# A feed-forward stage by seven half products for each pair of weight blocks, and an output projection in three token parts

## The chip, the core and the metric

The kernel runs on one core of a Trainium2 chip. The metric is device time in microseconds (us) of one execution; the kernel before took 2178.95 us (median of 3 runs, 2177.84 to 2180.29). TensorE (PE in the rows) multiplies, VectorE (DVE), ScalarE (ACT) and GpSimd (POOL) do elementwise work, and the queue of SyncE (SP) issues most transfers.

## The reference

One decoder layer in float32 for 1024 tokens of width 1024: token mixing (stick-breaking attention and retention, gated), a norm, attention into a memory of 256 rows, a norm, and this stage, the only one that the change rewrites:

```python
f = x @ w_ffn_in[l]                                   # 1024 -> 2 x 2816
ff = (jax.nn.silu(f[..., :FFN_HIDDEN]) * f[..., FFN_HIDDEN:]) @ w_ffn_out[l]
x = layer_norm(DN_ALPHA * x + ff, ln3_g[l], ln3_b[l])
```

## The kernel before

Everything is kept transposed: 128 channels on the partitions, tokens along the free dimension. `x_hi` and `x_lo` hold the 1024 channels as 8 tiles of [128, 1024]. Precision comes from splitting: a float32 value is a rounded part (hi, type fp32r) and the rest (lo), and each product is three matmuls, hi by lo, hi by hi and lo by hi, summed in PSUM. So each weight block of [128, 1024] (512 KB, 8 contraction tiles of 128x128) must be split before use. Before, POOL does this alone: `w_hi` by a multiplication with one (L280), `w_lo` by a subtraction (L283). Blocks arrive in a list in the order of use; SP loads them into two halves of `w_raw` (`stream`, L247 to L251), the next as soon as POOL has split the last of that slot.

The feed-forward stage has 22 hidden tiles of 128 channels, in three parts of 8, 7 and 7 (`FFN_PARTS`). For each hidden tile PE makes the gate half and the other half (2 blocks, each 8 contraction tiles by 2 token halves by 3 matmuls of 512 columns: 48), then ACT takes the silu from PSUM (L1176), DVE multiplies (L1607), ACT rounds to `a_hi` (L1178) and DVE subtracts to `a_lo` (L1609). After each part, 8 output blocks are multiplied with the part's hidden tiles in `a_hi` and `a_lo` and added to `acc`. That is 22 x 96 = 2112 matmuls inwards and 22 x 48 = 1056 outwards, all of 512 columns.

The norm before the stage (`n2`) has its totals summed by POOL and DVE, and its first half of tokens normalised, then the second: per 512 columns DVE centres (L1483) and scales (L1513), ACT applies gain and bias (L1076) and rounds (L1079), POOL subtracts (L301). PE starts the stage's first two blocks on parts as they come (`as_normed`, L722 to L726). The last norm (`n3`) does all 1024 tokens after the last matmul and stores 16 parts.

Of the kernel before, what the change touches and what calls it, by code (L numbers as in the profile page):

```python
# [26 lines left out]
ALU = mybir.AluOpType  # L27
# [5 lines left out]
P = 128  # L33
# [13 lines left out]
FFN_PARTS = (8, 7, 7)  # L47
# [13 lines left out]
RU, XU = 10, 6  # L61
STEPS = SB_PAIRS * QT
# [11 lines left out]
def layer_program(nc, xT, memT, stream8, stream7, params, rope, consts, ret_branch, outT):  # L74
    ctx = ExitStack()
    with ctx:
# [6 lines left out]

        x_hi = sb(ctx, "x_hi", [P, KT, SEQ], F32R)
# [10 lines left out]
        with ExitStack() as st:  # L95
            stick_set(st, 1)
        acc = sb(ctx, "acc", [P, KT, SEQ])
# [9 lines left out]
        ln_ones = sb(ctx, "ln_ones", [P, P], F32R)  # L107

# [36 lines left out]
        with ExitStack() as st:  # L145
# [7 lines left out]
            with ExitStack() as s2:  # L153
                silu_h = sb(s2, "silu_h", [P, SEQ])
                hidden = sb(s2, "hidden", [P, SEQ])

        with ExitStack() as st:
            y_out = sb(st, "y_out", [P, KT, SEQ])
        with ExitStack() as st:
# [5 lines left out]
            with ExitStack() as s2:  # L165
                ln_mean2, ln_rstd = sb(s2, "ln_mean2", [P, SEQ]), sb(s2, "ln_rstd", [P, SEQ])
                ln_t = sb(s2, "ln_t", [P, 4, HALF])
                ln_x = sb(s2, "ln_x", [P, 4, HALF])
                inv_col = sb(s2, "inv_col", [P, 2, 4])
# [48 lines left out]
        silu_read, hid_hi, hid_lo = sem("silu_read"), sem("hid_hi"), sem("hid_lo")  # L218
        scaled_odd, y_ready, out_stored = sem("scaled_odd"), sem("y_ready"), sem("out_stored")

        class Norm:

            def __init__(self, tag, residual):
# [3 lines left out]
                 self.centered, self.scaled) = (  # L227
# [3 lines left out]
                        "std", "turned", "inverted", "rstd", "centered", "scaled"))  # L231
                if residual:
                    self.a_hi, self.a_split, self.added, self.affine, self.hi, self.done = (
                        sem(f"{tag}_{n}") for n in ("a_hi", "a_split", "added", "affine", "hi", "done"))
                else:
                    self.rstd_copied = sem(f"{tag}_rstd_copied")

        n1, n2, n3 = Norm("n1", True), Norm("n2", True), Norm("n3", False)
# [5 lines left out]
        def _(sp):  # L244
# [20 lines left out]
            for q in range(2 * KT):  # L265
                hf, k = divmod(q, KT)
                sp.wait_ge(y_ready, q + 1)
                sp.dma_start(outT[k * P:(k + 1) * P, half(hf)], y_out[:, k, half(hf)]).then_inc(out_stored, 16)
            sp.wait_ge(out_stored, 16 * 2 * KT)
# [3 lines left out]
        def _(pool):  # L273
# [22 lines left out]
            def normed_lo(m, qs):  # L296

                for q in qs:
# [3 lines left out]
                                       ).then_inc(m.done, 1)  # L302

# [92 lines left out]
            residual(n2, U_MO, CH_MO, False, D, True)  # L396
            single(CH_FFN + 1)
            normed_lo(n2, range(2 * KT))
            split(CH_FFN + 2, 142 - CH_FFN - 2, 8 * P)
            split(142, 8, 7 * P)  # L400
            split(150, 14, 8 * P)
            split(164, 2, 7 * P)
            residual(n3, U_FFN + 60, 164, True, 7 * P, False)
            for q in range(1, 2 * KT, 2):
                hf = q // KT
                pool.wait_ge(n3.centered, q + 1)
                pool.wait_ge(n3.rstd_copied, hf + 1)
                pool.tensor_tensor(ln_t[:, q % 4, :], ln_t[:, q % 4, :], ln_rstd[:, half(hf)], ALU.mult
# [1320 lines left out]
```

## Time and profile before

| what | value |
|---|---|
| median of 3 runs | 2178.95 us |
| the profiled execution | 2180.05 us |
| its span (first to last instruction) | 2178.1 us |
| PE busy | 2059.9 us, 95% |
| POOL busy | 991.1 us, 46% |
| DVE busy | 825.3 us, 38% |
| ACT busy | 521.3 us, 24% |
| mean granted TensorE clock | 0.979 of full |
| transfers | 116.34 MB, mean 53 GB/s |

Busy time is a union over an engine's instructions. Successive matmuls overlap in the records: a matmul's own duration holds its way through the array, so the cost of one among many is the distance between two starts, not its duration. PEclk is the granted clock as a share of 2.4 GHz.

### The profile page before, as it was taken

How to read it: one execution, taken by the hardware profiler on the slowest of the kernel's cores; microseconds unless marked ns; L12 is line 12 of the kernel's file. 1: busy time of each engine (PE TensorE's matmuls, PEld its weight loads, DVE VectorE, ACT ScalarE, POOL GpSimd, SP SyncE). 2: the span in 40 equal slices, each digit the busy share in tenths (PEclk: the TensorE clock that was granted, in tenths of full speed). 3: DMA queues.
4: the chain of work that ended last, by engine and by line, in shares of the span. 5: the costliest groups of instructions: out<-in, count | busy, mean ns of one | idle time of the engine just before them, and what ended most of it. 6: DMA issues, size and time to landing. Idle time of an engine off the chain costs nothing.

```text
span 2178.1 us, 25755 instructions
## 1 busy us (share of the span) xinstructions
PE 2059.9 (95%) x10216; PEld 1702.2 (78%) x10216; DVE 825.3 (38%) x839; ACT 521.3 (24%) x732; POOL 991.1 (46%) x497
## 2 busy tenths in 40 slices
PE   7999999999999999999889989899999999999995
PEld 6888888788777777877678877678888888888884
DVE  5647466300166656144553324542122212112115
ACT  2413224210154555110252221151100000000013
POOL 4232242333354445346775426763344433433375
PEclk9999999999999999999999999899999999999997
DMA  4021020112100000311211111101111111111112
GB/s 187 24 84 65 32 86 20 68 67 77 48 22 28 20 20 30 116 49 39 68 59 58 67 39 39 49 29 48 48 48 48 48 48 44 53 48 48 45 42 77
DMA packets 33349, 116.34 MB, mean 53 GB/s; under 512 B 3728, under 2 KB 5136, under 8 KB 32272
## 3 DMA queue, kind: packets, MB, share of 16 engines
q1 hardware_dynamic: 27648, 93.56, 12.8%
q10 hardware_dynamic: 5648, 22.02, 2.7%
q8 instruction: 39, 0.64, 0.1%
q14 instruction: 14, 0.11, 0.0%
HBM read 107.18 MB, written 8.39 MB: 53 GB/s over the span
## 4 chain that ended last, share of the span: by engine, by line
PE 86%; DVE 8%; issue 2%; ACT 2%; POOL 1%; DMA 0%; POOLq 0%; DVEq 0%; ACTq 0%; SPq 0%
PE unit L437 23%; PE unit L443 23%; PE unit L441 23%; PE aux L602 2%; PE aux L608 2%; PE aux L606 2%; PE aux L415 2%; PE aux L417 1%; PE aux L416 1%; PE aux L562 1%; PE unit L551 1%; PE unit L415 1%; PE unit L417 1%; PE unit L416 1%; DVE ln_t L1483 1%
## 5 line engine op out<-in xcount | busy, mean ns | idle before, releaser
L280 POOL TENSOR_TENSOR w_hi<-w_raw,one 128x1024 fp32r<-128x1024 f32 (+1 forms) x130 | 245.1, 1885 | 888.7 <-PE unit L437 888.7
L437 PE MATMUL unit<-x_lo,w_hi 128*128 128x512 f32 x1440 | 563.3, 391 | 13.3 <-POOL w_lo L294 11.0
L443 PE MATMUL unit<-x_hi,w_lo 128*128 128x512 f32 x1440 | 561.3, 390 | 0.0
L441 PE MATMUL unit<-x_hi,w_hi 128*128 128x512 f32 x1440 | 561.1, 390 | 0.0
L437 PEld LDWEIGHTS unit<-x_lo,w_hi 128*128 128x128 f32 x1440 | 270.8, 188 | 72.5 <-POOL w_lo L294 11.0
L283 POOL TENSOR_TENSOR w_lo<-w_raw,w_hi 128x1024 fp32r<-128x1024 f32 (+1 forms) x130 | 322.1, 2478 | 10.2
L443 PEld LDWEIGHTS unit<-x_hi,w_lo 128*128 128x128 f32 x1440 | 270.7, 188 | 57.0
L441 PEld LDWEIGHTS unit<-x_hi,w_hi 128*128 128x128 f32 x1440 | 270.9, 188 | 55.5
L437 PE MATMUL unit<-a_lo,w_hi 128*128 128x512 f32 x608 | 240.2, 395 | 9.7 <-DVE a_lo L1395 9.7
L443 PE MATMUL unit<-a_hi,w_lo 128*128 128x512 f32 x608 | 239.2, 393 | 0.0
L441 PE MATMUL unit<-a_hi,w_hi 128*128 128x512 f32 x608 | 237.2, 390 | 0.0
L1607 DVE TENSOR_TENSOR hidden<-unit,silu_h 128x1024 f32<-128x1024 f32 x22 | 26.9, 1225 | 355.2 <-PE unit L443 355.2
L387 POOL TENSOR_TENSOR beta<-beta,stick 128x128 f32<-128x128 f32 (+7 forms) x64 | 77.1, 1205 | 151.6 <-DVE stick L1332 151.6
L437 PEld LDWEIGHTS unit<-a_lo,w_hi 128*128 128x128 f32 x608 | 114.6, 188 | 35.9 <-DVE a_lo L1395 9.1
L443 PEld LDWEIGHTS unit<-a_hi,w_lo 128*128 128x128 f32 x608 | 114.6, 188 | 26.1
L441 PEld LDWEIGHTS unit<-a_hi,w_hi 128*128 128x128 f32 x608 | 114.5, 188 | 25.6
L1332 DVE TENSOR_TENSOR_SCAN stick<-stick 128x128 f32<-128x128 f32 (+7 forms) x64 | 106.2, 1661 | 49.8 <-ACT stick L934 49.8
L1176 ACT ACTIVATE silu_h<-unit 128x1024 f32<-128x1024 f32 x22 | 22.6, 1027 | 331.2 <-PE unit L443 331.2
L1430 DVE SCALAR_TENSOR_TENSOR acc<-x_hi,unit 128x1024 f32 (+1 forms) x22 | 26.9, 1221 | 160.8 <-PE unit L443 160.8
L1178 ACT ACTIVATE a_hi<-hidden 128x1024 f32 x22 | 23.4, 1062 | 244.8 <-DVE hidden L1607 244.8
L602 PE MATMUL aux<-x_lo,w_hi 128*128 128x512 f32 x192 | 81.4, 424 | 0.3 <-DVE sk_lo L1347 0.3
L1609 DVE TENSOR_TENSOR a_lo<-hidden,a_hi 128x1024 f32 x22 | 66.6, 3028 | 29.4 <-ACT a_hi L1178 29.4
(258 smaller groups left out, 3252.2 us busy)
## 6 DMA issues: line engine op xcount, KB each, us to landing
w_raw<-stream SPq DMA_DIRECT2D x156, 512.0 KB, 3.3
rope_sb<-rope ACTq DMA_DIRECT2D x8, 1024.0 KB, 6.8
w_raw<-stream SPq DMA_DIRECT2D x16, 448.0 KB, 3.2
acc<-xT ACTq DMA_DIRECT2D x8, 512.0 KB, 9.5
ret_branch<-acc ACTq DMA_DIRECT2D x8, 512.0 KB, 2.6
acc<-ret_branch ACTq DMA_DIRECT2D x8, 512.0 KB, 7.9
outT<-y_out SPq DMA_DIRECT2D x16, 256.0 KB, 2.0
mem_raw<-memT ACTq DMA_DIRECT2D x1, 1024.0 KB, 5.4
```

The source lines that it names most:

```text
L280: pool.tensor_tensor(w_hi[s][:, 0:width], w_raw[:, s, 0:width], one[:].to_broadcast([P, width]), ALU.mult).then_inc(w_hi_done, 1)
L283: pool.tensor_tensor(w_lo[s][:, 0:width], w_raw[:, s, 0:width], f32(w_hi[s][:, 0:width]), ALU.subtract).then_inc(w_split, 1)
L387: pool.tensor_tensor(beta[g % 2][:, hd, 0:n], beta[g % 2][:, hd, 0:n], stick[:, hd, SEQ - n + 1:SEQ + 1], ALU.mult).then_inc(w_ready, 1)
L415: pe.matmul(out, l_hi, r_lo, start=start, stop=False, skip_group_check=True)
L416: pe.matmul(out, l_hi, r_hi, start=False, stop=False, skip_group_check=True)
L417: return pe.matmul(out, l_lo, r_hi, start=False, stop=stop, skip_group_check=True)
L437: x = pe.matmul(out, w_hi[s][:, wk], lo[:, k, cols], start=first, stop=False, skip_group_check=True)
L441: pe.matmul(out, w_hi[s][:, wk], hi[:, k, cols], start=False, stop=False, skip_group_check=True)
L443: last = pe.matmul(out, w_lo[s][:, wk], hi[:, k, cols], start=False, stop=(k == kts - 1), skip_group_check=True)
L602: x = pe.matmul(aux[:, 3, :], w_hi[s][:, wk], x_lo[:, k, half(hf)], start=(k == 0), stop=False, skip_group_check=True)
L1332: dve.tensor_tensor_scan(left[:, ::-1], left[:, ::-1], left[:, ::-1], 1.0, ALU.mult, ALU.bypass).then_inc(stick_scanned, 1)
L1609: dve.tensor_tensor(a_lo[:, bass.ds(j, 1), :].rearrange("p a t -> p (a t)"), hidden[:], f32(a_hi[:, bass.ds(j, 1), :].rearrange("p a t -> ...
```

## The change

The two weight blocks of hidden tile p (rows: gate, other) are cut into two contraction halves, and x into contraction halves and token halves. The 2 x 2 block product is made by Winograd's form of Strassen's method: seven products of [128 x 512] by [512 x 512] in place of eight, each 4 contraction tiles by 3 matmuls of 512 columns. Four of the seven weight forms are sums of quarters (`weight_sum`, DVE); four of the x forms are sums too and are made once, during the second norm (`turn`, `turn_hi_parts`, `turn_lo`): 16 sums on DVE, 16 roundings on ACT, 8 subtractions on POOL and 8 on DVE. The sum of two halves replaces one quarter of `x_hi`. Results are put together from PSUM: ACT copies four products to `held`, DVE makes four sums, ACT the silu, DVE the product, and each finished hidden tile is stored to a DRAM tensor `hidden_store`. The normed x is stored to `mid_x`.

The output projection is turned round: for token parts of 384, 384 and 256 columns, it goes over all 22 hidden tiles, with all eight output tiles open in the eight PSUM banks, 24 matmuls of the part's width for each hidden tile. `KEPT` is empty, so each part loads and splits each of the 22 output blocks anew: 66 loads of 512 KB, 66 roundings of 1024 columns on ACT (`out_hi`) and 66 subtractions on POOL (`out_lo`), in four slots (`W_FREE`). Hidden tiles are reloaded by part (`load_hidden`), rounded on ACT and subtracted on DVE, with two raw slots and four split ones. The last norm is done per part; that of the first two runs among the tiles of the next part, that of the last comes after the last matmul. POOL no longer rounds a weight block in this stage, and its weight block in the second norm's statistics becomes one subtraction of 512 columns. Loops over the stage are written out.

```diff
-FFN_PARTS = (8, 7, 7)
...
+A11, A12, S2, S1, S3, A22, S4 = range(7)
+PRODUCTS = [(0, A11), (1, A11), (0, A12), (1, A12)] + [(p, i) for p in range(FFN_TILES)
+                                                       for i in range(2 if p < 2 else 0, 7)]
+FORMS = len(PRODUCTS)
+AT = {product: f for f, product in enumerate(PRODUCTS)}
+SUMS = (S1, S2, S3, S4)
+RING = 4
...
+NORM_ORDER = [(0, k) for k in range(KT)] + [(1, k + j * QUART) for k in range(QUART) for j in range(2)]
+NORM_PARTS = [q for q, (hf, k) in enumerate(NORM_ORDER) if hf == 0 or k >= QUART]
...
+PARTS = ((0, 384), (384, 384), (768, 256))
+MOST = 384
+KEPT = ()
+W_FREE = 4
+TILES = [(t, k) for t in range(len(PARTS)) for k in range(FFN_TILES)]
+OUT_SPLITS = [(t, k) for t, k in TILES if t == 0 or k not in KEPT]
...
-            stream(stream8, 2, 2, 140, 8 * P)
-            stream(stream7, 0, 142, 8, 7 * P)
-            stream(stream8, 142, 150, 14, 8 * P)
-            stream(stream7, 8, 164, 8, 7 * P)
...
+            def load_out(m):
+                t, k = OUT_SPLITS[m]
+                if m >= 4:
+                    sp.wait_ge(w_split, CH_FFN + FORMS + m - 3)
+                sp.dma_start(out_raw(m), stream8[CH_FFN + 2 * FFN_TILES + k]).then_inc((o_loaded if m % 2 else w_loaded)[m // 2 % 2], 16)
+
+            def load_hidden(r):
+                t, k = TILES[r]
+                if r >= 2:
+                    sp.wait_ge(h_split, r - 1)
+                if t == 0:
+                    sp.wait_ge(hidden_stored[k % 2], 16 * (k // 2 + 1))
+                sp.dma_start(h_raw[:, r % 2, 0:PARTS[t][1]], hidden_store[k][:, columns(t)]).then_inc(h_loaded[r % 2], 16)
+
...
+                if (t, k) in ((0, 5), (0, 11), (2, 1)):
+                    load_residual({(0, 5): 0, (0, 11): 1, (2, 1): 2}[t, k])
...
+            def form_lo(f):
+                hi, lo = form_slot(f)
+                pool.wait_ge(w_hi_done, CH_FFN + f + 1)
+                pool.tensor_tensor(lo, form_source(*PRODUCTS[f]), f32(hi), ALU.subtract).then_inc(w_split, 1)
...
+            def out_lo(m):
+                hi, lo = out_weight(*OUT_SPLITS[m])
+                pool.wait_ge(w_hi_done, CH_FFN + FORMS + m + 1)
+                pool.tensor_tensor(lo, out_raw(m), f32(hi), ALU.subtract).then_inc(w_split, 1)
...
-            chunk, first, tiles = CH_FFN, U_FFN, 0
-            for part, kts in enumerate(FFN_PARTS):
-                if part == 0:
-                    as_normed(n2, chunk, first, mid=lambda: spread_rstd(n2, 1))
-                with pe.Fori(0 if part else 1, kts) as j:
-                    for g in range(2):
-                        u = free_unit(first, 2, j, g)
-                        project(j * 2 + (chunk + g), g, halves(u), x_hi, x_lo).then_inc(unit_ready, 1)
...
+            def product_part(p, i, k):
+                f = AT[p, i]
+                hi, lo = (w[:, k * P:(k + 1) * P] for w in form_slot(f))
+                xh, xl = x_form(i, k)
+                out, first, last = product_bank(p, i), k == 0 and i not in (S2, S3, S4), k == QUART - 1
+                pe.matmul(out, hi, xl, start=first, stop=False, skip_group_check=True)
+                pe.matmul(out, hi, xh, start=False, stop=False, skip_group_check=True)
+                x = pe.matmul(out, lo, xh, start=False, stop=last, skip_group_check=True)
+                if last:
+                    x.then_inc(unit_ready, 1)
+
...
+                if i == S2:
+                    pe.wait_ge(p1_held, p + 1)
...
+                        if i == S2:
+                            pe.wait_ge(t_split_pool, 2 * k + 2)
...
+            for p, i in PRODUCTS[4:]:
+                product(p, i)
...
+            for r, (t, k) in enumerate(TILES):
+                n = PARTS[t][1]
+                if t and k == 7:
+                    y_stats(t - 1)
+                hi, lo = out_weight(t, k)
+                pe.wait_ge(w_split, CH_FFN + FORMS + splits_before(t, k))
+                pe.wait_ge(h_split, r + 1)
...
+                    out, w = out_bank(o)[:, 0:n], slice(o * P, (o + 1) * P)
+                    pe.matmul(out, hi[:, w], h_lo[:, r % 4, 0:n], start=k == 0, stop=False, skip_group_check=True)
+                    pe.matmul(out, hi[:, w], h_hi[:, r % 4, 0:n], start=False, stop=False, skip_group_check=True)
+                    x = pe.matmul(out, lo[:, w], h_hi[:, r % 4, 0:n], start=False, stop=k == FFN_TILES - 1,
+                                  skip_group_check=True)
...
+            def out_hi(m):
+                t, k = OUT_SPLITS[m]
...
+                if k not in KEPT and loose_index(t, k) >= W_FREE:
+                    wait_tiles(act, tile_done, unit_ready, loose_tile(loose_index(t, k) - W_FREE) + 1)
+                act.activation(out_weight(t, k)[0], out_raw(m), ACT.Copy).then_inc(w_hi_done, 1)
...
+            def hidden_hi(r):
+                n = PARTS[TILES[r][0]][1]
+                act.wait_ge(h_loaded[r % 2], 16 * (r // 2 + 1))
+                if r >= 4:
+                    wait_tiles(act, tile_done, unit_ready, r - 3)
+                act.activation(h_hi[:, r % 4, 0:n], h_raw[:, r % 2, 0:n], ACT.Copy).then_inc(h_hi_done, 1)
...
+                if t and 13 <= k < 13 + KT:
+                    y_affine(t - 1, k - 13)
+                    if k > 13:
+                        y_store(t - 1, k - 14)
...
-                    dve.tensor_tensor(hidden[:], unit[:, 1, :], silu_h[:], ALU.mult).then_inc(unit_drained[1], 1)
...
+                b11, b21, b12, b22 = (acc[:, k + QUART * row, half(hf)] for hf in range(2) for row in range(2))
+                t1, t2, t3, t4 = (sum_slot(4 * k + j) for j in range(4))
+                for j, (out, l, r) in enumerate(((t1, b12, b11), (t2, b22, t1), (t3, b22, b12), (t4, t2, b21))):
...
+                    dve.tensor_tensor(out, l, r, ALU.subtract).then_inc(t_ready, 1)
...
+                    dve.tensor_tensor(t_lo[j + 1][:, k, :], sum_slot(4 * k + j), f32(t_hi[j + 1][:, k, :]), ALU.subtract
+                                      ).then_inc(t_split_dve, 1)
...
+                s1, s2 = form_source(p, S1), form_source(p, S2)
+                a11, a12, a21, a22 = (raw(p)[:, row, half(col)] for row in range(2) for col in range(2))
...
+                out, l, r, op = ((s1, a21, a22, ALU.add), (s2, s1, a11, ALU.subtract),
+                                 (form_source(p, S3), a11, a21, ALU.subtract),
+                                 (form_source(p, S4), a12, s2, ALU.subtract))[j]
+                dve.tensor_tensor(out, l, r, op).then_inc(form_summed, 1)
...
+            dve.wait_ge(mid_stored, 16 * 2 * KT)
+            dve.wait_ge(n2.done, len(NORM_PARTS))
...
+                if (p, i) == (1, A12):
+                    for j in range(4):
+                        weight_sum(0, j)
...
+                if t and k == 2:
+                    for o in range(KT):
+                        y_sum(t - 1, o)
```

What SP issues for the weights before, in the loop for 8 of the stage's blocks (`w_raw` is written from the list of blocks, ISA and REGISTER_ALU are the loop's waits and counts):

```order
L247 UNCONDITIONAL_BRANCH
L247 ISA
L251 ISA
L251 DMA w_raw<-stream8 128x1024
L250 REGISTER_ALU
L251 ISA
L251 DMA w_raw<-stream8 128x1024
```

And in the change, in the third token part (L380 is `load_out`, L388 is `load_hidden`):

```order
L388 DMA h_raw<-hidden_store 128x256
L380 DMA w_raw<-stream8 128x1024
L388 DMA h_raw<-hidden_store 128x256
L380 DMA w_raw<-stream8 128x1024
L388 DMA h_raw<-hidden_store 128x256
L380 DMA w_next<-stream8 128x1024
```

Between two loads of hidden tiles now stands a load of a weight block, in one queue.

ACT there, new in all its rows (L1510 `out_hi`, L1517 `hidden_hi`, L1585 and L1590 the last step of the norm of the part before, and its store):

```order
L1510 ACTIVATE w_early<-w_raw 128x1024
L1517 ACTIVATE h_hi<-h_raw 128x256
L1585 ACTIVATE y_out<-y_t,par 128x384
L1590 DMA outT<-y_out 128x384
L1510 ACTIVATE w_hi<-w_raw 128x1024
L1517 ACTIVATE h_hi<-h_raw 128x256
L1585 ACTIVATE y_out<-y_t,par 128x384
```

The rounding of a weight block stands behind that of the hidden tile before it.

DVE before, at the end of the second norm and the beginning of the stage:

```order
L1483 TENSOR_TENSOR ln_t<-acc,aux 128x512
L1513 TENSOR_TENSOR ln_t<-ln_t,aux 128x512
L1603 UNCONDITIONAL_BRANCH
L1603 ISA
L1605 REGISTER_ALU
L1607 TENSOR_TENSOR hidden<-unit,silu_h 128x1024
```

And in the change, after the last scaled part (L2049 and L2054 are the sums and the subtractions of the x forms, L2100 the weight sums of the first hidden tile):

```order
L2054 TENSOR_TENSOR t_lo<-sums_a,t_hi 128x512 x2
L2049 TENSOR_TENSOR sums_a<-acc 128x512
L2049 TENSOR_TENSOR sums_b<-acc,sums_a 128x512
L2049 TENSOR_TENSOR sums_b<-acc 128x512
L2049 TENSOR_TENSOR sums_a<-sums_b,acc 128x512
L2054 TENSOR_TENSOR t_lo<-sums_b,t_hi 128x512
L2054 TENSOR_TENSOR t_lo<-sums_a,t_hi 128x512
L2100 TENSOR_TENSOR sums_a<-w_raw 128x512
L2100 TENSOR_TENSOR sums_a<-sums_a,w_raw 128x512
```

Between the last scaled part and the stage now stand the sums of the x forms, and the first weight sums behind all of these.

## Rows read from the trace of the kernel before

**Rows 1.** The page: the span, and busy time, share and instructions of TensorE.

```profile
span 2178.1 us, 25755 instructions
...
PE 2059.9 (95%) x10216; PEld 1702.2 (78%) x10216; DVE 825.3 (38%) x839; ACT 521.3 (24%) x732; POOL 991.1 (46%) x497
```

**Rows 2.** Busy time by stretch; columns as its first row says.

```profile
core 0: us, PE busy (x) PEld busy (x) DVE busy (x) ACT busy (x) POOL busy (x), PEclk, DMA share, GB/s
1419.80:1442.00 22.20, 20.38 (x78) 15.22 (x78) 15.17 (x25) 20.80 (x30) 19.51 (x15) 0.88 0.00 1
1442.00:2142.30 700.30, 700.30 (x3079) 577.97 (x3080) 136.16 (x75) 63.84 (x60) 312.02 (x146) 1.00 0.14 47
2142.30:2178.10 35.80, 11.32 (x46) 7.80 (x44) 28.52 (x40) 17.95 (x26) 13.78 (x11) 0.68 0.31 117
```

**Rows 3.** Timeline of TensorE, norm to feed-forward stage: start us, us, instruction.

```profile
1419.81 0.77 PE L722 MATMUL unit<-x_lo,w_hi 128*128 128x512 f32 x1 [3.50 <-POOL x_lo L301]
1420.38 0.63 PE L724 MATMUL unit<-x_hi,w_hi 128*128 128x512 f32 x1
1420.81 0.63 PE L726 MATMUL unit<-x_hi,w_lo 128*128 128x512 f32 x1
```

**Rows 4.** The same, memory attention: first and last of 34 256-column matmuls.

```profile
1292.01 0.28 PE L417 MATMUL aux<-mk_hi,mq_lo 128*128 128x256 f32 x1
...
1295.96 0.28 PE L417 MATMUL aux<-mk_hi,mq_lo 128*128 128x256 f32 x1
```

**Rows 5.** Timeline of POOL, then of DVE, in the statistics of the second norm.

```profile
1404.68 2.37 POOL L308 TENSOR_TENSOR w_hi<-w_raw,one 128x1024 fp32r<-128x1024 f32 x1 [1.85 <-PE aux L671]
1407.13 2.67 POOL L311 TENSOR_TENSOR w_lo<-w_raw,w_hi 128x1024 fp32r<-128x1024 f32 x1
...
1405.33 2.27 DVE L1411 TENSOR_TENSOR total<-total,acc 128x512 f32<-128x512 f32 x1
1407.52 2.83 DVE L1415 TENSOR_TENSOR total_sq<-total_sq,square 128x512 f32<-128x512 f32 x1
```

**Rows 6.** Timeline of DVE, second norm: one part centred, scaled, the next centred.

```profile
1427.80 0.68 DVE L1483 TENSOR_TENSOR ln_t<-acc,aux 128x512 f32<-128x512 f32 x1
1428.58 0.69 DVE L1513 TENSOR_TENSOR ln_t<-ln_t,aux 128x512 f32<-128x512 f32 x1
```

**Rows 7.** Timeline of DVE, then of POOL, in the feed-forward stage.

```profile
1472.87 3.06 DVE L1609 TENSOR_TENSOR a_lo<-hidden,a_hi 128x1024 f32 x1 [1.34 <-ACT a_hi L1178]
...
1472.46 2.39 POOL L283 TENSOR_TENSOR w_lo<-w_raw,w_hi 128x1024 fp32r<-128x1024 f32 x1
```

**Rows 8.** Groups by shape, DVE: reciprocal, reduction, subtraction from PSUM.

```profile
L1256 DVE RECIPROCAL r_rstd<-r_mean 128x512 f32<-128x512 f32 x8 | 26.8, 3347 | 0.2
...
L1552 DVE TENSOR_REDUCE neg_max<-aux 128x4 f32<-128x1024 f32 x8 | 9.8, 1225 | 22.3 <-PE aux L417 22.3
...
L1338 DVE TENSOR_TENSOR wT_lo<-aux,wT_hi 128x384 fp32r<-128x384 f32 x8 | 4.3, 542 | 4.4 <-ACT wT_hi L939 4.4
```

**Rows 9.** Groups by shape: POOL, then ACT, three sizes.

```profile
L301 POOL TENSOR_TENSOR x_lo<-ln_x,x_hi 128x512 fp32r<-128x512 f32 x32 | 42.4, 1326 | 26.8 <-ACT x_hi L1079 24.9
...
L1178 ACT ACTIVATE a_hi<-hidden 128x1024 f32 x22 | 23.4, 1062 | 244.8 <-DVE hidden L1607 244.8
...
L1079 ACT ACTIVATE x_hi<-ln_x 128x512 fp32r<-128x512 f32 x32 | 20.2, 632 | 1.0
...
L893 ACT ACTIVATE rp_hi<-aux 128x384 fp32r<-128x384 f32 x8 | 3.9, 492 | 13.7 <-DVE diag L1270 13.7
```

**Rows 10.** Transfers: line, size, median us from issue to landing.

```profile
w_raw<-stream SPq DMA_DIRECT2D x156, 512.0 KB, 3.3
```

**Rows 11.** Busy time by stretch at the start of the span, columns as above.

```profile
10.00:20.00 10.00, 8.22 (x26) 6.29 (x27) 10.00 (x5) 7.03 (x7) 7.02 (x3) 1.00 0.92 344
```

**Rows 12.** Timeline at the end: last matmul of the stage, last normalised part.

```profile
2146.78 0.40 PE L443 MATMUL unit<-a_hi,w_lo 128*128 128x512 f32 x1
...
2174.84 0.81 ACT L1070 ACTIVATE y_out<-ln_t,par 128x512 f32<-128x512 f32 x1 [0.97 <-POOL ln_t L408]
```

More of the change, by code:

```diff
@@ L395, in _ @@
             split(CH_MEM + 4, CH_MO + 2 - CH_MEM - 4, 8 * P)
[L396 to L408, printed above, removed]
-                                   ).then_inc(scaled_odd, 1)
+            residual(n2, U_MO, CH_MO, False, D, False)
+            form_lo(0)
+            normed_parts()
+            for f in range(4, FORMS):
+                form_lo(f)
+            for m in range(len(OUT_SPLITS)):
+                out_lo(m)
         @block.tensor
@@ new lines, in _ @@
+            for j in range(2):
+                pe.wait_ge(unit_drained[j], U_MO // 2 + 4)
+            for i in (A11, A12):
+                for k in range(QUART):
+                    pe.wait_ge(n2.done, (i == A12) * QUART + k + 1)
+                    for p in range(2):
+                        if k == 0:
+                            pe.wait_ge(w_split, CH_FFN + AT[p, i] + 1)
+                        product_part(p, i, k)
+                    if i == A11 and k == 1:
+                        spread_rstd(n2, 1)
@@ L1185, in _ @@
+            act.activation(root_table[:, 2:3], one[:], ACT.Sqrt)
+            y_squares(2)
+            y_total_hi_parts(2)
+            y_copy_mean(2)
+            y_mean_square(2)
+            y_root(2)
+            for o in range(KT):
+                y_affine(2, o)
         @block.vector
@@ new lines, in _, with loose_index @@
+            for o in range(KT):
+                y_sum(2, o)
+            y_sum_chunks(2)
+            y_sum_squares(2)
+            y_total_lo_parts(2)
+            y_copy_square(2)
+            y_variance(2)
+            y_center(2, 0)
+            y_center(2, 1)
+            y_invert(2)
+            for o in range(KT):
+                if o >= 2:
+                    y_center(2, o)
+                y_scale(2, o)
+def loose_index(t, k):
+    per = FFN_TILES - len(KEPT)
+    return t * per + [j for j in range(FFN_TILES) if j not in KEPT].index(k)
@@ new lines, in loose_tile, with splits_before, wait_tiles @@
+def loose_tile(n):
+    per = FFN_TILES - len(KEPT)
+    return n // per * FFN_TILES + [j for j in range(FFN_TILES) if j not in KEPT][n % per]
+def splits_before(t, k):
+    return 1 + max(m for m, (a, b) in enumerate(OUT_SPLITS) if (a, b) == (t, k) or (k in KEPT and (a, b) == (0, k)))
+def wait_tiles(engine, tile_done, unit_ready, r):
+    t, k = divmod(r - 1, FFN_TILES)
+    if k == FFN_TILES - 1:
+        engine.wait_ge(unit_ready, U_FFN + FORMS + KT * (t + 1))
+    else:
+        engine.wait_ge(tile_done, t * (FFN_TILES - 1) + k + 1)
```

606 lines of the change are left out of this document (538 added, 68 removed).

## The prediction

> **What bounds the kernel now.** I read the page first: TensorE is busy 95% of the span [rows 1]. Then busy time by stretch: from 1442.0 to 2142.3 us, nearly the whole feed-forward stage, TensorE never rests, while DVE, ACT and POOL are busy 136, 64 and 312 of 700 us [rows 2]. So the stage costs what its matmuls cost: 3079 in 700.3 us, 0.2274 us from start to start. A matmul's own record is longer, about 0.4 us [rows 12], and may not be multiplied by a count. Two other places are not bound by TensorE: the second norm just before the stage (a granted clock of 0.88 in its last 22 us) and the last norm after it [rows 2].
>
> **Part 1, the statistics of the second norm.** There DVE takes 2.27 and 2.83 us for two additions of 512 columns, while POOL splits a whole weight block beside it [rows 5]; an operation of this size takes about 0.68 us alone [rows 6]. Why: a DVE subtraction of 1024 columns with both inputs in SBUF began 0.41 us after a POOL subtraction of 2.39 us and took 3.06 us, so it ended 1.08 us after POOL's [rows 7]. DVE had hardly moved until POOL was through. The two take turns, whole instructions at a time. The change takes the rounding and half of the subtraction away from POOL here, so I count 4 us earlier (at most 5.10 - 2 x 0.68 = 3.7 for the two, some more for the block before; at least 0).
>
> **Part 2, the beginning of the stage: dearer.** As before, TensorE can start on the first token half as it is normalised: 48 matmuls, of which those that fall in the half clock (1.2 GHz, start to start 0.43 us [rows 3]) cost double. They need about 17 us from 1416, so until 1433. The third product needs forms of x from the second half, and then weight sums that stand on DVE behind all of these. The second half starts with the centring at 1427.80 - 4 = 1423.8 [rows 6]. On DVE stand from there 8 pairs of centring and scaling, 0.78 + 0.61 = 1.39 us each (11.1 us), 16 sums, 8 subtractions and 2 weight sums, 26 x 0.61 = 15.9 us. POOL does 12 subtractions of 512 columns, 1.27 us each (the mean is 1.33 [rows 9]), and by rows 7 these and DVE's 26 with two SBUF inputs exclude each other: 15.2 us more if nothing overlaps. 1423.8 + 42.2 = 1466. What POOL hides behind the pairs (up to 5 us) I set against ACT's roundings, which DVE waits for twice (4 x 0.58 us each). Then ACT rounds three forms and frees the first product's bank, 4 x 0.63 = 2.5 us [rows 9], beside POOL's subtraction: the third product starts at **1469**. TensorE idles some 36 us. Bounds: 1454 if POOL costs nothing, 1474 if ACT's waits come in full.
>
> The Trainium skill (SBUF — State Buffer, Who interferes with whom) has this rule: a DVE instruction with two SBUF inputs and a GpSimd instruction that reads SBUF exclude one another, and the second fully blocks. By it the start is 1469, by engines that run side by side 1454. Rows 7 agree with it. The same section says that a reduction never contends.
>
> **Part 3, the products: cheaper.** 22 x 7 x 12 = 1848 matmuls of 512 columns in place of 2112; 48 are done before the wait, so 1800 x 0.2274 = 409.3 us. After the idle time the first 15 or so come at 0.43: 3 us. Beside each product (2.73 us) stand on ACT at most a copy, a silu and a rounding (1.9 us), on POOL one subtraction (1.27), on DVE 10 operations of 0.61 to 0.68 per seven products (6.6 of 19.1 us); with POOL's 8.9 the shared turn is taken 12.6 of 19.1 us. A form is made four products ahead. I count no wait; without that cover POOL would cost up to 1.9 us in a product. End: 1469 + 412 = **1881**.
>
> **Part 4, the output projection: here is the doubt.** Matmuls of 256 columns come 3.95 / 33 = 0.1197 us apart [rows 4]; 384 columns aren't shown in a long run, so I take the middle to 0.2274, 0.1736 (ends: 0.1197 and 0.2274; nearest is the line through both). Per hidden tile that is 24 matmuls, 4.17 us, and 2.87 us in the third part: 22 x (4.17 + 4.17 + 2.87) = 246.6 us, 6.5 more than 1056 x 0.2274. But around it runs a chain. SP issues the load of hidden tile r+1 behind that of weight block r+4, and this one waits until POOL has split block r. ACT rounds block r+2 only after it has rounded hidden tile r+1. POOL splits r+2 only then. So from split r to split r+2: 3.3 us for the weight block [rows 10], 0.5 for the hidden tile behind it in the same queue, 0.49 to round it, 1.06 to round the block [rows 9], 2.39 to split it [rows 7], and four handovers of 0.1: 8.1 us for two tiles. TensorE needs 8.33 for two in the first parts, so the chain just hides; in the third it needs 5.75, and the chain decides: (7.9 in place of 8.1, the hidden tile being smaller) 22 x 3.95 = 86.9 us, less 3.2 for three tiles split ahead. On the chain there also come, in the third part, 8 squares of 0.49 (3.9), a root with its table load (1.7) and 8 last steps with a store, 1.1 each on every second tile (4.4). That is 93.7; the sums that free the banks wait at its start behind a hidden tile that comes through the chain, a few us more: 96. In the first two parts 0.2 us per two tiles is all there is to catch up with: three loads of the residual in the same queue (1.5 MB at 344 GB/s [rows 11] is 4.6 us; two in the first part count 4 each, the third is in the 96), the start of the second part (7) and its statistics (3) stay nearly whole: 91.7 + 8 and 91.7 + 10. Sum **297 us**. Bounds: 252 if the loads come early enough everywhere (246.6 and the banks' handovers), 320 if the weight block takes 1 us longer than in rows 10 with the queue this full, on some 23 pairs of tiles that are bound or have no slack. I take 297, since 3.3 us is a median of 156.
>
> **Part 5, the last norm: cheaper.** Before, 2178.1 - 2147.0 = 31.1 us from the last matmul to the end [rows 12]. After, 256 columns: last bank's sum 0.4, two reductions over 8 x 256 (1.2 us for 1024 elements [rows 8], so 4.6), rounding and subtraction 0.8, sums on TensorE 1.2, copies, square, variance, root 1.8, reciprocal 3.35 / 2 = 1.7, eight pairs at 0.8 (6.4), last step 0.4, store and end 2178.1 - 2175.65 = 2.45, twelve handovers 1.2: **21 us** (17 to 26).
>
> **Sum.** 1881 + 297 + 21 = 2199 us of span; the execution lay 1.95 us over its span: **2201 us**. The profiled execution before took 2180.05, its median was 2178.95; I set mine beside the median, 1.0% more.
>
> **The rivals.**
> - **The loads hide.** For it: the third part moves 512 + 128 KB in 2.87 us, 229 GB/s, well under 344 [rows 11], and all buffers have two or four slots. Against it: the chain is one of waits, not of bytes. It decides as soon as a pair of tiles costs the chain less than TensorE, 5.75 us. Price: 297 - 252 = 45 us, so 2156, faster by 1.0%. The Trainium skill (DMA: Bandwidth & Descriptors, Rules for kernel authors) says that a transfer issued early and waited for late overlaps its fixed cost with compute; by that the time would be 2156. Whether these loads are issued early is the question, and no row of before shows it.
> - **Half and half.** The start is cheap (1454, 15 less) and the chain a little shorter (7.6 us, since the hidden tile lands with the block): third part 10 less, first parts 8 less. 2201 - 33 = 2168, 0.5% faster.
> - **The elementwise engines bind in the products too.** The turns of rows 7 cost a wait in some of 22 hidden tiles, 1.5 us each: 33 more, 2234. Against: 12.6 of 19.1 us.
> - **The products save nothing:** excluded; the matmul count is in the program.
>
> **How the numbers follow.** Forecast, with transfers up to 1 us slower: 0.57. Loads hide: 0.15. Half and half: 0.16. Elementwise engines bind: 0.12. Within the forecast a tenth of its chance lies within 0.2% of 2178.95 (what a measurement of this kernel can just tell from no change), another 0.02 comes from half and half. So faster 0.29, same 0.08, slower 0.63. The range of 8 in 10 is 2156 to 2232; the forecast's own is 2185 to 2222.
>
> **What would show it.** In the changed profile: a TensorE gap of some 30 us between 1430 and 1470, ended by a weight or x form; then 410 us without a gap; in the third part tiles 3.9 to 4.6 us apart in place of 2.87, waiting for `w_lo` (POOL) or `h_lo` (DVE) while SP waits for POOL and ACT for a transfer; 21 us after the last matmul. It is wrong if the third part's tiles come 2.9 us apart (loads hide), if the gap is under 20 us, or if the products show waits for POOL.

## The result, and the profile after the change

The changed kernel takes **2230.3 us** (median of 4 runs, 2227.5 to 2234.1) where the kernel before takes 2178.9 on the same chip. The ratio is 1.0237, with a 95% interval of 1.0219 to 1.0254. The forecast was 2201. The sign was right and the time lies in the range of 2156 to 2232, though outside the forecast's own (2185 to 2222): the loss is 51 us where 22 were forecast. The profiled execution took 2234.1 us, with a span of 2232.3; it is the longest of the four, 3.8 us above their median.

By stretch (columns as in [rows 2]): the start of the stage, the seven products, the three parts of the output projection, the last norm.

```profile
1421.00:1474.00 53.00, 15.47 (x57) 11.78 (x58) 43.71 (x55) 31.32 (x51) 33.99 (x25) 0.64 0.20 76
1473.70:1892.00 418.30, 418.29 (x1800) 340.46 (x1801) 204.68 (x216) 162.75 (x281) 214.49 (x150) 0.99 0.23 83
1892.00:2006.00 114.00, 97.52 (x530) 96.00 (x528) 25.43 (x28) 36.44 (x49) 59.24 (x25) 0.94 0.57 187
2006.00:2116.00 110.00, 97.99 (x540) 97.38 (x540) 45.36 (x56) 44.45 (x68) 52.98 (x22) 0.93 0.54 169
2116.00:2209.40 93.40, 74.13 (x540) 72.06 (x540) 53.94 (x59) 37.98 (x69) 46.51 (x19) 0.88 0.41 127
2209.40:2232.30 22.90, 1.97 (x8) 1.78 (x8) 16.73 (x25) 7.45 (x16) 0.00 (x0) 0.60 0.14 46
```

[Rows 2] had one unbroken stretch of 700 us here, with the last norm behind it. Now there are 418 us without a gap (0.2324 us per matmul, where [rows 2] had 0.2274; without the 14 matmuls at the half clock behind the first gap it is 0.2309), and then 317 us in which TensorE rests for some 48 and the granted clock is 0.88 to 0.94. What it waits for from 1380 us on (total, times, longest):

```profile
PE unit L1000 <- ACT held L1476: 35.4, 1, 35.4
PE unit L1080 <- DVE h_lo L2136: 21.7, 14, 4.5
PE unit L1080 <- DVE y_acc L2179: 14.5, 2, 7.4
PE aux L1080 <- ACT y_total L1568: 11.3, 2, 6.4
```

The first row is the gap before the third product. The other three are the output stage: hidden tiles that come late, the two changes of part, and the mean that a later tile waits for. That a load stands behind all three is shown by the experiment on SP's order. In the same stage ScalarE waits for hidden tiles, and SP waits for GpSimd's splits before it may issue (waits of ScalarE, then of SP's queue, 1880 to 2210 us):

```profile
ACT h_hi L1517 <- DMA h_raw<-hidden_store: 167.3, 57, 9.1
...
SPq L380 <- POOL w_turns L490: 120.5, 29, 11.5
SPq L380 <- POOL w_lo L490: 62.2, 15, 8.6
SPq L380 <- POOL w_early L490: 55.2, 15, 10.7
```

SP's own timeline in the first part shows the rhythm:

```profile
1932.02 0.33 SPq L380 DMA_DIRECT2D w_raw<-stream  x1
1932.46 0.38 SPq L388 DMA_DIRECT2D h_raw<-hidden_store  x1
1937.51 0.33 SPq L380 DMA_DIRECT2D w_raw<-stream  x1
1937.94 0.38 SPq L388 DMA_DIRECT2D h_raw<-hidden_store  x1
1940.17 0.33 SPq L380 DMA_DIRECT2D w_next<-stream  x1
```

No hidden load here goes out alone: each leaves 0.4 us after the weight block that it stands behind, and two blocks take 1940.17 - 1932.02 = 8.15 us. The prediction had worked out 8.1. So the chain is there, and at its tightest it has the size forecast. Over the stage it is longer: from one weight load to the next but one the median is 8.3 us in the first part (25 pairs) and 9.2 in the second and third (22 and 13). What the forecast lacked is seen where TensorE starts again after a gap, here tile 2 of the first part:

```profile
1900.52 0.33 PE L1082 MATMUL aux<-h_hi,w_lo 128*128 128x384 f32 x1
1905.33 0.66 PE L1080 MATMUL unit<-h_lo,w_turns 128*128 128x384 f32 x1 [4.47 <-DVE h_lo L2136]
1905.78 0.52 PE L1081 MATMUL unit<-h_hi,w_turns 128*128 128x384 f32 x1
1906.10 0.52 PE L1082 MATMUL unit<-h_hi,w_turns 128*128 128x384 f32 x1
...
1909.94 0.36 PE L1082 MATMUL unit<-h_hi,w_turns 128*128 128x384 f32 x1
1910.14 0.34 PE L1080 MATMUL unit<-h_lo,w_turns 128*128 128x384 f32 x1
1910.32 0.34 PE L1081 MATMUL unit<-h_hi,w_turns 128*128 128x384 f32 x1
```

After 4.47 us without work 14 matmuls start 0.32 us apart, the lower level of 1.2 GHz, and only then 0.175. The third part starts in the same way, with 25 matmuls 0.21 us apart where 0.12 is the pitch of 256 columns:

```profile
2116.13 0.56 PE L1080 MATMUL unit<-h_lo,w_early 128*128 128x256 f32 x1 [7.15 <-DVE y_acc L2179]
2116.48 0.42 PE L1081 MATMUL unit<-h_hi,w_early 128*128 128x256 f32 x1
2116.70 0.41 PE L1082 MATMUL unit<-h_hi,w_early 128*128 128x256 f32 x1
```

The 1584 matmuls of the stage take 316.6 us from first to last start. Over the forecast's 246.4 (its pitches of 0.1736 and 0.1197) these are 53 us in 19 distances of over 0.6 us, **13 us in 113 distances at the lower level**, 1.5 us since 384 columns come 0.1751 us apart and not 0.1736, and 2.7 us in other distances, most of them the first behind a gap. The forecast had 50.4 us of idle time (297 - 246.6) and nothing for the lower level.

The Trainium skill (TensorE: Matmul & The Clock Gate, "Wait — 56ns, not 53.3ns?") gives for matmuls in a row the number of columns over 1.2 GHz at the lower level, and over 2.4 GHz plus 2.5 ns at the upper. Worked out from it, an estimate, that is 0.32 us for 384 columns at the lower level and 0.2158 for 512 at the upper. The first agrees with this trace; at the upper level no kind of matmul with 512 columns here came closer together than 0.2262 on average, so there the measurement decides.

### The profile page after: what moved, and what is told of

It is laid out like the page before. It is cut to its first block, busy times and chain, and to the rows that moved or that the text cites. A ratio compares the mean times of both kernels' runs of the same rounds, so it can differ in the third digit from the quotient of the medians.

```text
span 2232.3 us, 27030 instructions
## 1 busy us (share of the span) xinstructions
PE 2038.7 (91%) x10488; PEld 1722.0 (77%) x10488; DVE 1025.5 (46%) x1132; ACT 738.1 (33%) x1146; POOL 1041.6 (47%) x561
## 4 chain that ended last, share of the span: by engine, by line
PE 73%; DVE 10%; DMA 7%; ACT 4%; POOL 3%; issue 3%; SPq 0%; ACTq 0%; DVEq 0%; POOLq 0%
PE unit L618 12%; PE unit L624 12%; PE unit L622 12%; DMA h_raw<-hidden_store 6%; PE unit L1000 4%; PE unit L1002 4%; PE unit L1001 4%; PE aux L1001 3%; PE aux L1000 3%; PE aux L1002 3%; PE aux L783 2%; PE aux L789 2%; PE aux L787 2%; PE aux L596 1%; PE aux L598 1%
## 5 line engine op out<-in xcount | busy, mean ns | idle before, releaser
L437 POOL TENSOR_TENSOR w_hi<-w_raw,one 128x1024 fp32r<-128x1024 f32 x70 | 133.3, 1904 | 524.1 <-PE unit L618 524.1
L618 PE MATMUL unit<-x_lo,w_hi 128*128 128x512 f32 x752 | 295.3, 393 | 12.6 <-POOL w_lo L451 11.4
L622 PE MATMUL unit<-x_hi,w_hi 128*128 128x512 f32 x752 | 294.1, 391 | 0.0
L624 PE MATMUL unit<-x_hi,w_lo 128*128 128x512 f32 x752 | 294.0, 391 | 0.0
L440 POOL TENSOR_TENSOR w_lo<-w_raw,w_hi 128x1024 fp32r<-128x1024 f32 x70 | 173.9, 2485 | 5.5
L618 PEld LDWEIGHTS unit<-x_lo,w_hi 128*128 128x128 f32 x752 | 141.8, 189 | 43.4 <-POOL w_lo L451 11.4
L622 PEld LDWEIGHTS unit<-x_hi,w_hi 128*128 128x128 f32 x752 | 141.8, 189 | 29.2
L618 PE MATMUL unit<-a_lo,w_hi 128*128 128x512 f32 x256 | 102.0, 399 | 9.6 <-DVE a_lo L1832 9.6
L1000 PE MATMUL unit<-t_lo,w_hi 128*128 128x512 f32 x176 | 70.8, 402 | 35.4 <-ACT held L1476 35.4
L624 PE MATMUL unit<-a_hi,w_lo 128*128 128x512 f32 x256 | 101.7, 397 | 0.0
L622 PE MATMUL unit<-a_hi,w_hi 128*128 128x512 f32 x256 | 100.7, 393 | 0.0
L1517 ACT ACTIVATE h_hi<-h_raw 128x384 fp32r<-128x384 f32 (+1 forms) x66 | 32.0, 487 | 167.4 <-DMA h_raw<-hidden_store 167.3
```

The costliest lines, as they stand in the source:

```text
L437: pool.tensor_tensor(w_hi[s][:, 0:width], w_raw[:, s, 0:width], one[:].to_broadcast([P, width]), ALU.mult).then_inc(w_hi_done, 1)
L440: pool.tensor_tensor(w_lo[s][:, 0:width], w_raw[:, s, 0:width], f32(w_hi[s][:, 0:width]), ALU.subtract).then_inc(w_split, 1)
L618: x = pe.matmul(out, w_hi[s][:, wk], lo[:, k, cols], start=first, stop=False, skip_group_check=True)
L622: pe.matmul(out, w_hi[s][:, wk], hi[:, k, cols], start=False, stop=False, skip_group_check=True)
L624: last = pe.matmul(out, w_lo[s][:, wk], hi[:, k, cols], start=False, stop=(k == kts - 1), skip_group_check=True)
L1000: pe.matmul(out, hi, xl, start=first, stop=False, skip_group_check=True)
```

## The experiments

Twelve kernels ran, each timed against the kernel before on the same chip. They go after two causes: where tiles lie in SBUF, and how the output stage is fed. The gap at the start of the stage and the combinations follow.

### The place of tiles in SBUF

The change moves `inv_col` (32 bytes a partition) ahead of all tiles of the upper region. The mixing projection's matmuls, which the change doesn't touch, had become slower. The first try restored a multiple of 64 bytes:

```diff
         inv_col = sb(ctx, "inv_col", [P, 2, 4])
+        pad = sb(ctx, "pad", [P, 8])
```

> Only the place of tensors in SBUF changes: 32 more bytes a partition stand behind inv_col, so that the tiles of the mixing projections (a_hi, a_lo) and the turned inputs of the half products (t2 to t4) begin at a multiple of 64 bytes again, as before the change. Theory A (a moving operand that begins 32 bytes off costs TensorE time): product matmuls that read t tiles fall from 0.234-0.236 us to the 0.227 of those that read x tiles, the seven-product stage from 418.3 to about 410, the mixing projections from 0.2333 to 0.229, the program from 2230 to 2215-2220. Rival (the longer pitch comes from the other engines' traffic in that stage): pitches and time as in the change, 2228-2232.

Measured: 2227.2 us, ratio 1.0213 (1.0196 to 1.0230), between what theory and rival said. Matmuls that read t tiles into `unit` went only from 0.2337-0.2358 to 0.2321-0.2333 us, and a_hi and a_lo stayed at 0.233. Multiples of 64 are not the rule, so theory A fell in that form; but the pitches had moved with nothing but addresses. The same 32 bytes in the kernel before:

```diff
         ln_ones = sb(ctx, "ln_ones", [P, P], F32R)
+        pad = sb(ctx, "pad", [P, 8])
```

> The kernel before with 32 bytes a partition put in behind ln_ones, where inv_col stands in the changed kernel: the tiles a_hi, a_lo, sbo_hi and all behind them sit as they do after the change, nothing else differs. Theory A2 (the address of a moving operand alone moves the pitch, by amounts that no rule seen so far gives: in the first experiment 32 bytes more did not bring the mixing projections back): a_hi and a_lo matmuls go from 0.2277-0.2305 us to the 0.2315-0.2343 of the changed kernel, x tiles stay at 0.227, the time grows by 2-4 us. Rival (the pitch upstream comes from other edits of the change): pitches and time within 0.5 us.

Measured: **2189.1 us, ratio 1.0044 (1.0027 to 1.0061)**: 10 us for 32 unused bytes, more than the 2 to 4 expected. The 1824 matmuls that read a_hi or a_lo, 1056 of them the old output projection's, come 0.2334 us apart on average where they came 0.2290 apart, 8 us in all. In the 600 us from 1500 to 2100, 2624 matmuls start and not 2640. The offsets seen so far suggested 128 modulo 256, where x_hi and x_lo lie:

```diff
         inv_col = sb(ctx, "inv_col", [P, 2, 4])
+        pad = sb(ctx, "pad", [P, 40])
```

> The changed kernel with 160 bytes a partition behind inv_col, so that every tile of the upper region begins at 128 modulo 256, as x_hi and x_lo do; nothing else differs. So far: operands at 128 gave 0.227 us a matmul, at 192 (before) 0.228-0.231, at 224 (the change) 0.232-0.237, at 0 (first experiment) 0.233. Theory A3 (the start address modulo 256 sets it): mixing projections and products at 0.227 throughout, the seven-product stage 408-411 us instead of 418, the program 2208-2216. Rival (the lower region is fast, the upper one slow whatever the offset): pitches stay at 0.230 or more, 2224-2232.

Measured: **2215.5 us, ratio 1.0170 (1.0153 to 1.0187)**, 14.8 us less than the change. The products' stretch of this kernel, beside the 418.30 us above for the same work:

```profile
1465.50:1876.20 410.70, 410.70 (x1801) 339.93 (x1801) 204.70 (x216) 162.72 (x281) 213.44 (x150) 0.99 0.24 85
```

The other engines' busy times are the same to half a per cent, so it is no traffic that went away. The stage's first matmul comes at 1414.3 us. In eight profiles without this pad it came between 1418.2 and 1423.3, in the three with it between 1414.3 and 1415.2. The kernel before, with 192 bytes (`[P, 48]`) where the second experiment had 32:

> The kernel before with the upper region at the same 128 modulo 256 (192 bytes behind ln_ones). Theory A3: its a_hi and a_lo matmuls (608 of each of three kinds, 0.2266 to 0.2306 us) fall to 0.227, 3-4 us less in them and as much in the retention and memory projections: 2172-2177. Rival: 2178-2182, or up to 2190 as with 32 bytes.

Measured: 2176.4 us, ratio 0.9984 (0.9974 to 0.9994), a small gain as expected. Pitches (mean distance of starts, us) over the six kernels, by the offset of the upper region modulo 256:

| Tile read, weights | before, 192 | before, 224 | before, 128 | change, 224 | change, 0 | change, 128 |
|---|---|---|---|---|---|---|
| a_lo, w_hi | 0.2306 | 0.2323 | 0.2267 | 0.2342 | 0.2327 | 0.2272 |
| a_hi, w_hi | 0.2266 | 0.2318 | 0.2267 | 0.2315 | 0.2329 | 0.2272 |
| a_hi, w_lo | 0.2298 | 0.2360 | 0.2269 | 0.2343 | 0.2330 | 0.2262 |
| t_hi, w_lo (`unit`) | - | - | - | 0.2358 | 0.2333 | 0.2270 |
| x_lo, w_hi (`unit`; never moved) | 0.2272 | 0.2270 | 0.2268 | 0.2269 | 0.2271 | 0.2267 |

Shown: the address of the moving operand (the one that streams through the array) sets the pitch here, by up to 4%. The pads move other engines' tiles too, but the matmuls on x tiles in the same stretches keep their pitch. Open: whether 128 modulo 256 counts by itself or because w_hi and w_lo lie there too, as they do in all six.

### The feed of the output stage

**SP's order.** The hidden tile of the next step goes ahead of the weight block; all else stays.

```diff
             for r, (t, k) in enumerate(TILES):
-                if r >= 2:
-                    load_hidden(r)
+                if 1 <= r < len(TILES) - 1:
+                    load_hidden(r + 1)
```

> Only SP's order in the output stage changes: the hidden tile of step r+1 is loaded ahead of the weight tile of step r+4, not behind it. Theory B (the queue makes each hidden tile wait until POOL has split a weight tile, a chain of about 8.1 us for two tiles; the stalls of parts 1 and 2 and most small gaps of part 3 are its lag): ScalarE's wait for hidden tiles falls from 167 us to under 60, the output stage from 317 to 280-295, the time to 2195-2210. Rival C (transfers share a limited rate, or the elementwise engines bind by themselves): the wait changes its name and the stage stays within 5 us of 317, the time 2225-2232.

Measured: **2187.4 us (10 runs), ratio 1.0032 (1.0022 to 1.0041)**, 43 us less than the change, more than theory B asked for. The output stage, and ScalarE's waits in it:

```profile
1887.80:2159.80 272.00, 258.83 (x1609) 255.96 (x1607) 188.36 (x140) 118.43 (x185) 158.89 (x65) 0.97 0.57 190
```

```profile
ACT w_turns L1510 <- PE aux L1082: 40.7, 18, 2.8
ACT h_hi L1517 <- DMA h_raw<-hidden_store: 38.6, 21, 7.5
ACT w_hi L1510 <- PE aux L1082: 19.0, 8, 2.9
ACT w_early L1510 <- PE aux L1082: 18.4, 8, 2.8
```

The stage took 317.40 before this edit (TensorE busy 269.64, clock 0.92). ScalarE's wait for hidden tiles falls from 167.3 to 38.6 us, and what it now waits for most is TensorE to free a weight slot: the feed is ahead. The same bytes go at 190 GB/s, where the change had 163, so rival C falls: the transfers could go faster. TensorE's three waits of the stage go from 47.5 to 13.0 us:

```profile
PE unit L1080 <- DVE h_lo L2136: 11.6, 6, 5.6
...
PE unit L1080 <- DVE y_acc L2179: 0.8, 2, 0.4
PE aux L1080 <- ACT y_total L1568: 0.6, 1, 0.6
```

The waits at the changes of part and for the late mean nearly vanish with it though neither was edited: each stood on its engine behind a hidden tile. The rule weighed in the prediction (the Trainium skill, DMA: Bandwidth & Descriptors, Rules for kernel authors) is that a transfer issued early hides its fixed cost. The pair agrees with it: issued a step earlier, the hidden tiles cost ScalarE 38.6 us of waiting and not 167.3. In the change they were not issued early.

**Fewer loads.** Nine of 22 weight tiles stay split in SBUF.

```diff
-KEPT = ()
+KEPT = (1, 3, 6, 8, 11, 13, 16, 18, 21)
```

> Nine of the 22 output weight tiles are kept split in SBUF for parts 2 and 3, so that 48 tiles are loaded and split and not 66. If the reloading and splitting is what the output stage pays for: part 1 as in the change (114 us), part 2 from 110 to 98-102, part 3 from 93 to 75-80, the time 2195-2210. If only the lag of hidden tiles and the fixed places of the statistics cost there: under 8 us less, 2222-2230.

Measured: 2195.9 us, ratio 1.0075 (1.0058 to 1.0092), 34 us less. The stage takes 283.6 us; parts 2 and 3 take 99 and 76 us, as the first case has it, and part 1 falls too, from 114 to 108, which it did not foresee. A kept tile waits for no load, so the chain has fewer links; but that doesn't yet tell the load's own cost from its place in the queue.

**Residual sums ahead of the hidden tile.**

```diff
+                if t and k == 2:
+                    for o in range(KT):
+                        y_sum(t - 1, o)
                 if r >= 2:
                     hidden_lo(r)
-                if t and k == 2:
-                    for o in range(KT):
-                        y_sum(t - 1, o)
```

> Only DVE's order changes: the eight residual sums of a finished part stand ahead of the hidden tile of step k=2 of the next, not behind it. Theory D (the 7.35 and 7.15 us in which TensorE stands between parts come from DVE being held at that hidden tile): both gaps fall to 1.5 us or less, the time by 10-13 us to 2217-2221. Rival (the sums themselves or the residual load are late, or the feed of tiles is the limit and takes the time back within the part): gaps of over 4 us stay or come back in the next tiles, the time 2226-2232.

Measured: 2224.4 us, ratio 1.0203 (1.0186 to 1.0221), 6 us less, between theory D and its rival. TensorE's waits:

```profile
PE unit L1080 <- DVE h_lo L2136: 29.1, 17, 7.9
PE aux L1080 <- ACT y_total L1568: 12.3, 2, 6.3
...
PE unit L1080 <- DVE y_acc L2179: 2.3, 2, 2.1
```

The 14.5 us at the changes of part are 2.3 now, and 7.4 of the 12.2 gained come back as waits for hidden tiles. Theory D names the place, not the cause: more than half of it is paid elsewhere while the feed sets the pace.

**Both, and all four.**

> Both edits at once: hidden tile first in SP's queue, nine tiles kept. Alone they gave 43 and 34 us. If the reload mattered only because it sat in the hidden tiles' chain, the second adds little once the first is made: 2180-2187. If the reload also costs by itself (DMA, ScalarE and GpSimd time in parts 2 and 3): the output stage goes from 271.5 us to about 258, the time to 2170-2176. TensorE's own pace is 247 us for the stage.

Measured: 2174.1 us, ratio 0.9973 (0.9961 to 0.9984). The stage falls from 272 to 259 us, as in the second case:

```profile
1892.30:2151.60 259.30, 253.96 (x1609) 253.41 (x1608) 122.76 (x140) 99.76 (x165) 113.31 (x46) 0.99 0.50 163
```

So the 18 reloads that `KEPT` spares cost 13 us by themselves and 34 behind the bad order.

> All four edits (place of the tiles, hidden tile first, nine tiles kept, residual sums ahead of the hidden tile). If the four gains were separate they would add to -86 us, 2144; since TensorE needs 247 us for the output stage, at most 24 us are left beyond the hidden-first kernel. Expected 2166-2174, below the kernel before (2179.6); the rival, that the feed of tiles still binds: 2180-2187.

Measured: 2168.1 us, ratio 0.9946 (0.9929 to 0.9962), as expected. The place of the tiles is that of the first experiment here, 32 bytes and not 160.

### The gap at the start of the stage

On top of hidden-first, GpSimd's `turn_lo` is emptied, and DVE's makes its two subtractions as well:

```diff
             def turn_lo(k):
+                for j, (hi, lo) in enumerate(((x_hi[:, k, half(1)], x_lo[:, k, half(1)]),
+                                              (t_hi[2][:, k, :], t_lo[2][:, k, :]))):
+                    dve.wait_ge(t_hi_done, 4 * k + j + 1)
+                    dve.tensor_tensor(lo, sum_slot(4 * k + j), f32(hi), ALU.subtract).then_inc(t_split_pool, 1)
                 for j in (2, 3):
```

> On top of hidden-first: the eight low parts of the turned inputs that GpSimd makes in the start gap (x_lo and t2_lo) are made by DVE. Theory E (the 35.4 us gap is set by DVE, and operations that run beside a GpSimd one take 1.75 us instead of 0.69): DVE gets 8 operations of 0.61 us more and loses about 10 stretches of 1 us, the gap falls to 28-31 us, the time to 2180-2184. Rival (GpSimd's work is parallel work, DVE just gets more): the gap grows to 39-41 us, the time to 2191-2193.

Measured: 2180.5 us (10 runs), ratio 1.0003 (0.9993 to 1.0013), 7 us less than hidden-first alone; the gap falls from 35.4 to 30.9 us. DVE, then GpSimd, in the gap of the hidden-first kernel, and DVE in this one:

```profile
1454.49 0.69 DVE L2049 TENSOR_TENSOR sums_b<-acc,sums_b 128x512 f32<-128x512 f32 x1
1455.10 0.68 DVE L2049 TENSOR_TENSOR sums_a<-acc 128x512 f32<-128x512 f32 x1
1455.70 1.76 DVE L2049 TENSOR_TENSOR sums_a<-sums_b,acc 128x512 f32<-128x512 f32 x1
...
1455.13 1.78 POOL L485 TENSOR_TENSOR x_lo<-sums_b,x_hi 128x512 fp32r<-128x512 f32 x1 [1.29 <-ACT x_hi L1448]
```

```profile
1458.55 0.68 DVE L2046 TENSOR_TENSOR sums_a<-acc 128x512 f32<-128x512 f32 x1
1459.15 0.68 DVE L2046 TENSOR_TENSOR sums_a<-sums_b,acc 128x512 f32<-128x512 f32 x1
1459.76 0.68 DVE L2052 TENSOR_TENSOR x_lo<-sums_b,x_hi 128x512 fp32r<-128x512 f32 x1
```

A DVE operation that meets one of GpSimd's takes 1.76 us, one that doesn't 0.68. DVE does 8 more and is through sooner. This is the exclusion of [rows 7], which set Part 2 of the prediction, and what the Trainium skill (SBUF — State Buffer, Who interferes with whom) states of two SBUF inputs; the trace agrees. The gap accounts for 4.5 us. In the two profiles the output stage is 2.5 us shorter as well (271.5 and 269.0 us from first to last matmul), which nothing in the edit explains; whether it belongs to the 7 us is open.

### Two causes away, and everything together

With the pad of 160 bytes and SP's order alone (all 66 loads and splits stay):

> Only the two causes found are taken away from the change: 160 bytes behind inv_col and the hidden tile first in SP's queue. The three parts, all 66 loads and splits and the places of sums and statistics stay. If the two are independent: 2230 - 43 - 15 = 2172 (2169-2175), below the kernel before (2179), which would mean that the half products and the three parts were worth their cost all along and that queue order and placement turned a gain into a loss. If they overlap: 2180-2186.

Measured: **2170.9 us, ratio 0.9957 (0.9940 to 0.9973)**. The two add: 14.8 + 42.9 = 57.7 expected, 59.4 measured.

> All that helped, together: the upper region at 128 modulo 256, hidden tile first, nine tiles kept, residual sums early, the turned low parts on DVE. From the 2168 of the four edits together: -4.5 us of start gap (30.9 for 35.4), and by theory A3 another 8-14 us: 2150-2157. Without A3: 2162-2166.

Measured: **2153.5 us, ratio 0.9884 (0.9868 to 0.9901)**, 25 us faster than the kernel before and 77 than the change. Its stretches: start, products, output stage, last norm.

```profile
1415.20:1461.50 46.30, 14.66 (x56) 11.05 (x56) 40.25 (x61) 29.45 (x48) 18.74 (x15) 0.65 0.23 85
1461.50:1871.70 410.20, 409.57 (x1800) 339.08 (x1800) 204.83 (x216) 164.31 (x284) 216.45 (x152) 1.00 0.24 85
1871.70:2128.30 256.60, 251.13 (x1609) 250.55 (x1608) 122.02 (x140) 99.75 (x165) 112.52 (x46) 0.99 0.50 165
2128.30:2151.50 23.20, 2.07 (x9) 1.78 (x8) 17.09 (x26) 7.80 (x17) 0.00 (x0) 0.55 0.14 46
```

## Why the prediction was wrong in size, point by point

The span of the profiled execution came out 33.3 us over the sum (2232.3 for 2199); by the median it would be 29:

| Step | Forecast | Measured | Over the sum |
|---|---|---|---|
| Third product starts | 1469 | 1473.7 | +4.7 |
| Products, to the end of the 1800 | 412 | 418.3 | +6.3 |
| Output projection | 297 | 317.1 | +20.1 |
| Last norm | 21 | 23.2 | +2.2 |

- **Part 1 and the start** (1416 for the first matmul, 1422.0 measured): the 4 us were there. From the last matmul of the memory's output projection to the first of the stage the kernel before takes 18.4 us and the change 13.8, 4.6 less. They were paid away before. The 32 bytes account for some 3: that last matmul comes at 1401.5 us before, at 1403.9 with the 32 bytes alone, and at 1404.4 at the earliest in the change and its variants at the same addresses. That term was missing: I had no row for what a moved tile costs. The other 4 us, up to the 1408.2 of the profiled execution, are scatter: the stretch with the first norm and the memory attention took 237.4 to 241.9 us in six kernels that are the same up to there. With the upper region at 128 modulo 256 the first matmul of the stage comes at 1414.3 to 1415.2.
- **Part 2** was right. The gap was put at some 36 us and is 35.4; the late start is inherited.
- **Part 3: the step that failed is "1800 x 0.2274"**, the pitch of other tiles at other addresses. At the full clock it measured 0.2309, and 0.2267 once the tiles lay at 128 modulo 256; the 3 us for slow matmuls at the start were right (14 of them, 2.9 us). No wait was counted and none came. So the rival of 0.12 (elementwise engines bind in the products) is out, though its 2234 lies closest to the time measured.
- **Part 4: the chain was there and the idle time was right, 53 us for 50.4. The step that failed is that matmuls between the gaps were all counted at the full clock.** 113 distances came at the lower level and cost 13 us. The prediction had charged 3 us for just this behind the gap of Part 2, from [rows 3], and nothing behind the gaps that it forecast itself. The total of the idle time is closer than its parts: with each change of part counted to the part that begins, it is 10, 14 and 29 us, where 8, 10 and 33 were forecast. "The chain just hides" was a little too kind to the first two parts.
- **Part 5**: 2.2 us too little, within its range.
- **The rival that the loads hide** did not occur. Its price was 45 us, and the hidden-first kernel, which takes the chain apart with one change of order, gains 43. That the two are so close is partly luck: the price was 297 - 252 and the gain is from 317 to 272, with 20 us that were not forecast at either end.

The two failed steps are 15 us of placement (2230.3 - 2215.5, in Parts 1, 3 and 4 together) and 13 us of clock, close to the 29 by which the forecast missed. With the tiles at 128 modulo 256 the span is 14.2 us over the sum: the start comes 3.5 us early and the products take 1.3 less than forecast, while the output stage is 17.0 over and the last norm 2.0. Of the 17.0, 11 are the clock (13 in the change), and some 3 each are more idle time and the first distances behind gaps; that these and the early start nearly cancel is luck. The clock's share is read from the trace; no run took the clock away and kept the gaps. It fell when the gaps did: in the stage 113 slow distances in the change, 44 with hidden-first, 12 in the last kernel.

## What to carry to other kernels

A load that a queue holds behind another load inherits the other's wait: before a chain is accepted, ask which of the two the consumer needs first. A forecast gap on TensorE should be charged twice, once for the wait and once for the matmuls behind it at the half clock: in the change that was 1 to 2.3 us more behind each of the seven waits of 2.2 us and over. And when an edit shifts buffers, compare the start-to-start distance of matmuls that the edit doesn't touch before blaming its logic.

## What the runs showed of the hardware that I had not expected

- A 512-column fp32r matmul with its moving operand at 128 modulo 256 bytes came every 0.2262 to 0.2272 us, at 192 every 0.2266 to 0.2306, at 0 every 0.2327 to 0.2333, at 224 every 0.2315 to 0.2360. The three kinds on a tiles averaged 0.2269 at most, 0.2290, 0.2329 and 0.2334. For the kernel before, 32 unused bytes made 10 us.
- Gaps on TensorE didn't all cost the same at the clock. In the output stage of the change seven waits were followed by matmuls at the lower level: 2.17 us by 11, 3.87 by 23, 4.47 by 14, 4.89 by 17, 6.36 by 22, 7.15 by 25, 7.35 by 8. Behind the shorter ones, up to 1.85 us, none was slow beyond the first. Each of the seven cost 1.0 to 2.3 us at the clock; the length of the wait alone didn't tell how much: a wait of 2.94 us in the hidden-first kernel was followed by 18 slow matmuls, one of 2.87 at the same place of the kernel with the low parts on DVE by none.
- The first matmul of the stage came anywhere from 1418.2 to 1423.3 us in six kernels whose program and addresses up to there are the same: a shift of 5 us there is no finding by a single profile. Most of it arose in the stretch with the first norm and the memory attention.
